# Four modulation tiles per load in the head of a two-layer trunk, and the mixed unit's tiles one by one

## The chip, the cores and the metric

The kernel runs on one core of a Trainium2 chip. The time is the device time of one execution in microseconds (us). The kernel before has a median of 2176.46 us over three runs (2176.29 to 2176.57).

The core has TensorE (PE; its weight loads are shown as PEld), VectorE (DVE), ScalarE (ACT), GpSimd (POOL) and SyncE (SP). In this kernel all loads and stores are issued by SyncE, and 16 DMA engines carry them.

## What is computed

A trunk of two layers on 256 tokens of width 2048, in float32. Each layer has a mixer (layer 0 pools over windows, layer 1 is a gated linear recurrence) and a SwiGLU FFN, and both are modulated by six vectors that come from one conditioning vector c:

```
cond = jax.nn.silu(c)
for layer in range(DEPTH):
    mod = cond @ w_ada[layer] + b_ada[layer]
    sh_m, sc_m, g_m, sh_f, sc_f, g_f = jnp.split(mod[:, None, :], N_MOD, axis=-1)
    h = rms_norm(x, norm_mix_gain[layer]) * (1.0 + sc_m) + sh_m
    ...
    x = x + g_m * y
    h = rms_norm(x, norm_ffn_gain[layer]) * (1.0 + sc_f) + sh_f
    x = x + g_f * swiglu(h, w_ffn_in[layer], w_ffn_out[layer])
return rms_norm(x, final_gain)
```

`w_ada` has 2048 rows and 12288 columns per layer, 100.7 MB each, as much as a large part of the other weights. It is used for one row vector, so its cost is bringing it in and multiplying it once.

## The kernel before

**Units.** `w_ada` is cut into units of 2048 rows x 1024 columns (half a section; the mixed units take 512 columns of the FFN's shift and 512 of its scale). A unit is 16 tiles of 128 rows x 1024 columns, 512 KB each; tile k holds rows 128k to 128k+127. Seven units are worked off in the head, ahead of the main loop, in the order of `HEAD`: scale, shift, scale, shift of the first mixer (units 0 to 3), its gate in two halves (units 4, 5) and the mixed unit (unit 6). Seventeen more are spread through the main loop (`BEHIND`).

**Who works on a unit.** In the head, TensorE takes the first tiles of each unit (`PE_LOADS`: 7, 7, 7, 6, 8, 8, 9 of the 16) in `multiply_loads`, line 665: two products per tile, which the trace shows as four rows of 128x512. VectorE folds the rest in `fold`, lines 1343 (first) and 1346 (the others), each as tile times cond plus the accumulator. Line 1340 adds TensorE's row to VectorE's accumulator. Then TensorE sums over the partitions (`sum_columns`, line 672, after `head_columns`, line 683, or `reduce_unit`, line 699, for the gates) and ScalarE copies the result (line 990 or 997). Between the units stand the pooling matmuls (lines 766, 767), the products with the pooling weights (lines 637 to 639) and the residual updates. The main loop begins with the first FFN product, at 178.25 us in the trace.

**The ring of tiles.** The head's tiles go to a ring of 16 slots (tile n to slot n mod 16): slots 0 to 3 are `ada`, slots 4 to 15 are `ada_head`. SyncE issues the loads in program order. For each pair of tiles (n even) it waits until both slots are free (`ada_free`, counted up by TensorE or VectorE when they have read a tile) and issues one DMA of 1 MB, line 429. In HBM the two tiles lie so that each partition's 8 KB are contiguous. One semaphore per pair tells the arrival; both tiles' consumers wait for it (`ada_arrived`). SyncE's order in the head: parameters; unit 0 (the bias rows `brows` behind its fourth tile); x; units 1 and 2; two pooling weight tiles; unit 3; two more; unit 4; four more and `pscale`; unit 5; two FFN weight tiles; unit 6. Behind the head, tiles come one by one to `ada`, line 425, 4 KB per partition, from the same array, between the weight tiles (line 405), which are 512 KB and contiguous.

## Time and profile before

| | |
|---|---|
| median of three runs | 2176.46 us (2176.29 to 2176.57) |
| the profiled execution | 2179.37 us, span 2177.7 us |
| TensorE busy | 2130.3 us, 98% of the span |
| VectorE busy | 1641.1 us, 75% |
| ScalarE busy | 998.0 us, 46% |
| moved by DMA | 574.34 MB, mean 264 GB/s |
| the head (0 to 178 us) | DMA share 0.97, 399 GB/s; TensorE busy 152.41 us |

Busy times are of one execution. Times in the traces are us from the span's start. The DMA share is the mean busy share of the 16 engines, and it stands at 1.01 or 1.02 where they never pause, since packets of an engine overlap a little. The granted clock is TensorE's, as a share of 2.4 GHz.

### The profile page before, as it was taken

The numbers are of one execution on the slowest core, as the hardware profiler recorded it, in microseconds if no ns is written. First come the engines' busy times: TensorE is split into PE (matmuls) and PEld (weight loads), VectorE is DVE, ScalarE is ACT, GpSimd is POOL, SyncE is SP. The second block draws the span as 40 slices with busy tenths as digits, with TensorE's granted clock in tenths as the row PEclk, the third lists the DMA queues.
The fourth block names the chain that finished last, engine by engine and source line by source line (L and its number), as shares of the span: only waits on it lengthen the run. The fifth ranks groups of instructions, "written<-read, shape, count | busy, mean of one in ns | idle before, by whom it ended". The sixth has DMA issues, their size and how long they took to land.

```text
span 2177.7 us, 24635 instructions
## 1 busy us (share of the span) xinstructions
PE 2130.3 (98%) x9513; PEld 1724.8 (79%) x9513; DVE 1641.1 (75%) x1685; ACT 998.0 (46%) x1116; POOL 21.0 (1%) x89
## 2 busy tenths in 40 slices
PE   7999999999999999999999999999999999999997
PEld 3557887888888888878888888878888888888886
DVE  5779899999988887769787887677756666546644
ACT  2324544444444334455655566554454444444433
POOL 1000000000000000010000000000000000000000
PEclk9999999999999999999999999999999999999999
DMA  9998898988899998756666664578856556558664
GB/s 383 418 418 336 326 345 295 322 319 315 311 339 331 340 338 290 251 181 231 217 202 213 222 199 160 191 281 300 280 185 192 185 182 187 193 188 297 236 216 136
DMA packets 149105, 574.34 MB, mean 264 GB/s; under 512 B 16662, under 2 KB 16854, under 8 KB 141308
## 3 DMA queue, kind: packets, MB, share of 16 engines
q1 hardware_dynamic: 148988, 572.77, 74.6%
q8 instruction: 75, 1.23, 0.2%
q14 instruction: 42, 0.34, 0.0%
HBM read 570.60 MB, written 2.10 MB: 263 GB/s over the span
## 4 chain that ended last, share of the span: by engine, by line
PE 91%; DVE 4%; issue 2%; DMA 1%; ACT 1%; SPq 0%; DVEq 0%; ACTq 0%
PE prod L637 28%; PE prod L639 28%; PE prod L638 28%; DVE acc L1346 2%; PE modp L665 2%; PE small L708 1%; DMA ada<-in_ada_sections 1%; PE small L880 1%; PE modp L672 1%; DMA ada_head<-in_ada_sections 1%; PE modp L699 1%; PE small L855 0%; DVE part_value L1642 0%; PE small L901 0%; PE small L865 0%
## 5 line engine op out<-in xcount | busy, mean ns | idle before, releaser
L964 ACT ACTIVATE w_hi<-raw 128x1024 fp32r<-128x1024 f32 x696 | 736.0, 1061 | 988.9 <-PE prod L639 908.3
L1297 DVE TENSOR_TENSOR w_lo<-raw,w_hi 128x1024 fp32r<-128x1024 f32 x696 | 848.3, 1222 | 420.7 <-ACT w_hi L964 419.2
L637 PE MATMUL prod<-w_hi,h_hi 128*128 128x512 f32 x2072 | 818.9, 395 | 4.9 <-issue 1.9
L639 PE MATMUL prod<-w_hi,h_lo 128*128 128x512 f32 x2072 | 808.3, 390 | 0.0
L638 PE MATMUL prod<-w_lo,h_hi 128*128 128x512 f32 x2072 | 808.1, 390 | 0.0
L637 PEld LDWEIGHTS prod<-w_hi,h_hi 128*128 128x128 f32 x2072 | 390.1, 188 | 86.7 <-issue 3.1
L639 PEld LDWEIGHTS prod<-w_hi,h_lo 128*128 128x128 f32 x2072 | 389.9, 188 | 82.0
L638 PEld LDWEIGHTS prod<-w_lo,h_hi 128*128 128x128 f32 x2072 | 390.3, 188 | 79.0 <-issue 1.0
L1346 DVE SCALAR_TENSOR_TENSOR acc<-ada,cond,acc 128x1024 f32<-128x1024 f32 x255 | 326.1, 1279 | 0.4
L637 PE MATMUL prod<-w_hi,g_hi 128*128 128x512 f32 x688 | 268.8, 391 | 0.0
L639 PE MATMUL prod<-w_hi,g_lo 128*128 128x512 f32 x688 | 267.7, 389 | 0.0
L638 PE MATMUL prod<-w_lo,g_hi 128*128 128x512 f32 x688 | 267.7, 389 | 0.0
L637 PEld LDWEIGHTS prod<-w_hi,g_hi 128*128 128x128 f32 x688 | 129.2, 188 | 27.3 <-issue 0.5
L638 PEld LDWEIGHTS prod<-w_lo,g_hi 128*128 128x128 f32 x688 | 129.2, 188 | 27.1 <-issue 0.5
L639 PEld LDWEIGHTS prod<-w_hi,g_lo 128*128 128x128 f32 x688 | 129.1, 188 | 26.7
L665 PE MATMUL modp<-ada,cond_rows 128*128 128x512 f32 x112 | 57.3, 671 | 10.3 <-DMA brows<-in_b_ada 6.8
L665 PEld LDWEIGHTS modp<-ada,cond_rows 128*128 128x128 f32 x112 | 23.7, 217 | 40.5 <-issue 35.1
L708 PE MATMUL small<-ident,tok 128*128 128x128 f32 x272 | 37.3, 282 | 7.0 <-issue 4.8
L708 PEld LDWEIGHTS small<-ident,tok 128*128 128x128 f32 x272 | 32.8, 145 | 13.8 <-issue 6.9
L665 PE MATMUL modp<-ada_head,cond_rows 128*128 128x512 f32 x96 | 42.3, 592 | 0.0
L1346 DVE SCALAR_TENSOR_TENSOR acc<-ada_head,cond,acc 128x1024 f32<-128x1024 f32 x29 | 37.2, 1284 | 4.4 <-DMA ada_head<-in_ada_sections 2.0
L1046 ACT ACTIVATE feat<-small,mod,gain 128x256 f32<-128x256 f32 x48 | 23.4, 563 | 29.5 <-PE small L708 27.0
(196 smaller groups left out, 1051.9 us busy)
## 6 DMA issues: line engine op xcount, KB each, us to landing
raw<-in_w_ffn_in SPq DMA_DIRECT2D x352, 512.0 KB, 4.6
ada<-in_ada_sections SPq DMA_DIRECT2D x256, 512.0 KB, 5.9
raw<-in_w_ffn_out SPq DMA_DIRECT2D x176, 512.0 KB, 4.3
raw<-in_hgrn_w_in SPq DMA_DIRECT2D x128, 512.0 KB, 3.6
ada_head<-in_ada_sections SPq DMA_DIRECT2D x36, 1024.0 KB, 15.7
raw<-in_hgrn_w_out SPq DMA_DIRECT2D x32, 512.0 KB, 3.5
ada<-in_ada_sections SPq DMA_DIRECT2D x12, 1024.0 KB, 12.0
ada<-in_ada_mixed SPq DMA_DIRECT2D x16, 512.0 KB, 7.3
```

The source lines that it names most:

```text
L637: pe.matmul(o, hi[:, k, ts], wh, start=(begin and s == 0), stop=False)
L638: pe.matmul(o, hi[:, k, ts], wl, start=False, stop=False)
L639: mm = pe.matmul(o, lo[:, k, ts], wh, start=False, stop=(end and s == n - 1))
L665: mm = pe.matmul(modp[:, o], cond_rows[:, k], ada_buffer(slot)[:, o * CH:(o + 1) * CH], start=(k == 0), stop=(in_columns(u) and k == n_row ...
L672: mm = pe.matmul(modp[:, 0, j:j + 1], a[:, j * P:(j + 1) * P], ones[:, 0:1], start=False, stop=(j == UB - 1))
L699: mm = pe.matmul(modp[:, o], ones[:, :], a[:, o * CH:(o + 1) * CH], start=not begun, stop=True)
L708: mm = pe.transpose(small[half][:, o:o + P], block_of(tb, 2 * half + j), ident[:, :])
L880: mm = pe.matmul(small[b][:, o:o + P], kdec[:, b, pair, ts], kdec[:, b, 2 + pair, ts], start=True, stop=True)
L964: act.activation(w_hi[:, slot], raw[:, r], ACT.Copy).then_inc(hi_ready, 1)
L1046: ins = act.activation(feat[:, half, j], small[half][:, j * S:(j + 1) * S], ACT.Identity, bias=shifts[:, k:k + 1], scale=gains[:, k:k + 1])
L1297: dve.tensor_tensor(w_lo[:, slot], raw[:, r], w_hi[:, slot], ALU.subtract).then_inc(lo_ready, 1)
L1346: ins = dve.scalar_tensor_tensor(a, ada_buffer(slot), cond[:, k:k + 1], a, ALU.mult, ALU.add)
```

## The change

For units 0 to 5 of the head one load brings four tiles (2 MB, 16 KB per partition in one piece) instead of two. SyncE waits for four free slots before it issues, and consumers of any of the four tiles wait for the whole load. The mixed unit (unit 6) is loaded tile by tile, 4 KB per partition, as the units behind the head are; each of its tiles has its own semaphore. For this the arrays in HBM are laid out in groups of four tiles, so that a single tile's rows lie 16 KB apart from partition to partition (8 KB before). That holds for the 16 tiles of every single-tile unit, in the main loop too.

```
-    sections = w.reshape(L, D // (2 * P), 2, P, 6, 2, D // 2).transpose(0, 4, 5, 1, 3, 2, 6)
-    mixed = w[0, :, 3 * D:5 * D].reshape(D // (2 * P), 2, P, 2, D // CH, CH)[:, :, :, :, 0:2].transpose(4, 0, 2, 1, 3, 5)
-    return sections, mixed.reshape(2, D // (2 * P), P, 2, 2 * CH)
+    sections = w.reshape(L, D // (4 * P), 4, P, 6, 2, D // 2).transpose(0, 4, 5, 1, 3, 2, 6)
+    mixed = w[0, :, 3 * D:5 * D].reshape(D // (4 * P), 4, P, 2, D // CH, CH)[:, :, :, :, 0:2].transpose(4, 0, 2, 1, 3, 5)
+    return sections, mixed.reshape(2, D // (4 * P), P, 4, 2 * CH)
...
-            if n < len(HEAD) * KD:
-                slot -= slot % 2
-            elif slot % 2:
-                before -= len(HEAD) * KD // ADA_HEAD
+            if n < (len(HEAD) - 1) * KD:
+                slot -= slot % 4
+            elif slot % 4:
+                before -= len(HEAD) - 1
...
-                if u >= len(HEAD):
+                if u >= len(HEAD) - 1:
                     sp.wait_ge(ada_free[slot], before)
-                    sp.dma_start(ada_buffer(slot), tiles[k // 2, :, k % 2]).then_inc(ada_loaded[slot], 16)
-                elif k % 2 == 0:
-                    for tile in range(2 if before else 0):
+                    sp.dma_start(ada_buffer(slot), tiles[k // 4, :, k % 4]).then_inc(ada_loaded[slot], 16)
+                elif k % 4 == 0:
+                    for tile in range(4 if before else 0):
                         sp.wait_ge(ada_free[slot + tile], before)
-                    sp.dma_start(ada_pair(slot).rearrange("p k n -> p (k n)"),
-                                 tiles[k // 2].rearrange("p k n -> p (k n)")).then_inc(ada_loaded[slot], 16)
+                    sp.dma_start(ada_four(slot).rearrange("p k n -> p (k n)"),
+                                 tiles[k // 4].rearrange("p k n -> p (k n)")).then_inc(ada_loaded[slot], 16)
```

No instruction of TensorE, VectorE or ScalarE is added, removed or moved; what they wait for changes. On SyncE the loads are merged.

VectorE in unit 0, the folds of tiles 7 to 14 and the row that adds TensorE's sum. `ada_loadedN` is the semaphore of the load that brings slot N and its followers, `ada_freeN` tells that slot N has been read. Before:

```order
L1343 TENSOR_SCALAR acc<-ada_head,cond 128x1024 [waits ada_loaded6,cond_ready]
L1346 SCALAR_TENSOR_TENSOR acc<-ada_head,cond,acc 128x1024 [waits ada_free7,ada_loaded8]
L1346 SCALAR_TENSOR_TENSOR acc<-ada_head,cond,acc 128x1024 [waits ada_free8,ada_loaded8]
L1346 SCALAR_TENSOR_TENSOR acc<-ada_head,cond,acc 128x1024 [waits ada_free9,ada_loaded10]
L1346 SCALAR_TENSOR_TENSOR acc<-ada_head,cond,acc 128x1024 [waits ada_free10,ada_loaded10]
L1346 SCALAR_TENSOR_TENSOR acc<-ada_head,cond,acc 128x1024 [waits ada_free11,ada_loaded12]
```

The same folds now:

```order
L1343 TENSOR_SCALAR acc<-ada_head,cond 128x1024 [waits ada_loaded4,cond_ready]
L1346 SCALAR_TENSOR_TENSOR acc<-ada_head,cond,acc 128x1024 [waits ada_free7,ada_loaded8]
L1346 SCALAR_TENSOR_TENSOR acc<-ada_head,cond,acc 128x1024 [waits ada_free8,ada_loaded8]
L1346 SCALAR_TENSOR_TENSOR acc<-ada_head,cond,acc 128x1024 [waits ada_free9,ada_loaded8]
L1346 SCALAR_TENSOR_TENSOR acc<-ada_head,cond,acc 128x1024 [waits ada_free10,ada_loaded8]
L1346 SCALAR_TENSOR_TENSOR acc<-ada_head,cond,acc 128x1024 [waits ada_free11,ada_loaded12]
```

The folds are the same and in the same order; the wait of tile 8 (`ada_loaded8`) is now for a load of tiles 8 to 11, and tile 7 waits for tiles 4 to 7.

SyncE between unit 2's last loads and unit 3's first ones, before:

```order
L429 DMA ada_head<-in_ada_sections 128x2048 [waits ada_free13,ada_free12]
L429 DMA ada_head<-in_ada_sections 128x2048 [waits ada_free15,ada_free14]
L405 DMA raw<-in_pool_w 128x1024 x2
L429 DMA ada<-in_ada_sections 128x2048 [waits ada_free1,ada_free0]
L429 DMA ada<-in_ada_sections 128x2048 [waits ada_free3,ada_free2]
L429 DMA ada_head<-in_ada_sections 128x2048 [waits ada_free5,ada_free4]
```

And now:

```order
L429 DMA ada_head<-in_ada_sections 128x4096 [waits ada_free14,ada_free15,ada_free13,ada_free12]
L405 DMA raw<-in_pool_w 128x1024 x2
L429 DMA ada<-in_ada_sections 128x4096 [waits ada_free2,ada_free3,ada_free1,ada_free0]
L429 DMA ada_head<-in_ada_sections 128x4096 [waits ada_free6,ada_free7,ada_free5,ada_free4]
L429 DMA ada_head<-in_ada_sections 128x4096 [waits ada_free10,ada_free11,ada_free9,ada_free8]
```

Two issues have become one, and the first load of unit 3 waits for slots 0 to 3, where it waited for 0 and 1.

## Rows read from the trace of the kernel before

**Rows 1.** The page: the span, and busy time of each engine.
```profile
span 2177.7 us, 24635 instructions
...
PE 2130.3 (98%) x9513; PEld 1724.8 (79%) x9513; DVE 1641.1 (75%) x1685; ACT 998.0 (46%) x1116; POOL 21.0 (1%) x89
```

**Rows 2.** Stretches (us): busy time per engine, granted clock, DMA share, rate.
```profile
core 0: us, PE busy (x) PEld busy (x) DVE busy (x) ACT busy (x) POOL busy (x), PEclk, DMA share, GB/s
...
178.00:460.00 282.00, 278.75 (x1226) 227.46 (x1227) 263.67 (x260) 134.12 (x140) 0.00 (x0) 0.99 0.88 324
...
20.00:40.00 20.00, 16.09 (x47) 9.89 (x46) 11.36 (x10) 5.31 (x16) 0.00 (x0) 0.77 1.01 421
60.00:78.00 18.00, 15.28 (x50) 7.96 (x49) 16.75 (x23) 2.11 (x2) 0.00 (x0) 1.00 1.01 418
...
280.00:300.00 20.00, 20.00 (x90) 16.30 (x89) 18.49 (x21) 8.35 (x8) 0.00 (x0) 1.00 1.01 393
282.00:298.00 16.00, 16.00 (x72) 12.97 (x71) 14.49 (x17) 6.33 (x7) 0.00 (x0) 1.00 1.02 399
```

**Rows 3.** Instructions in order of time, VectorE, head: start, us, what, [idle before].
```profile
18.57 9.62 DVE L1346 SCALAR_TENSOR_TENSOR acc<-ada_head,cond,acc 128x1024 f32<-128x1024 f32 x7 [1.67 <-DMA ada_head<-in_ada_sections]
...
43.50 1.29 DVE L1346 SCALAR_TENSOR_TENSOR feat<-ada_head,cond,feat 128x1024 f32<-128x1024 f32 x1 [1.20 <-DMA ada_head<-in_ada_sections]
...
55.45 1.28 DVE L1346 SCALAR_TENSOR_TENSOR feat<-ada_head,cond,feat 128x1024 f32<-128x1024 f32 x1
```

**Rows 4.** Instructions in order of time, TensorE, head.
```profile
30.86 3.57 PE L672 MATMUL modp<-ones,acc 128*128 128x1 f32 x16 [0.93 <-DVE acc L1346]
...
36.00 9.57 PE L665 MATMUL modp<-ada,cond_rows 128*128 128x512 f32 x16
...
57.44 0.39 PE L683 MATMUL modp<-ident,brows 64*128 64x8 f32 x2
...
62.27 7.03 PE L665 MATMUL modp<-ada,cond_rows 128*128 128x512 f32 x16
...
127.15 7.11 PE L665 MATMUL modp<-ada,cond_rows 128*128 128x512 f32 x16 [1.92 <-DMA ada<-in_ada_sections]
...
154.87 7.13 PE L665 MATMUL modp<-ada,cond_rows 128*128 128x512 f32 x16 [1.11 <-ACT gate L990]
...
178.25 0.77 PE L637 MATMUL prod<-w_hi,h_hi 128*128 128x512 f32 x1 [1.90 <-issue]
```

**Rows 5.** The chain that ended last, in order of time: start, us, what.
```profile
107.81 19.21 DMA ada<-in_ada_sections
```

**Rows 6.** Instructions in order of time, ScalarE, before unit 5.
```profile
125.27 1.02 ACT L990 ACTIVATE gate<-modp 128x1024 f32<-128x1024 f32 x1 [21.29 <-PE modp L699]
```

**Rows 7.** The DMA view of the whole span: instruction queue, and a lone load's landing.
```profile
q8 instruction: 75, 1.23, 0.2%
...
raw<-in_hgrn_w_out SPq DMA_DIRECT2D x32, 512.0 KB, 3.5
```

**Rows 8.** Stretches of half granted clock, columns as in rows 2.
```profile
30.70:41.00 10.30, 10.14 (x30) 7.31 (x31) 1.31 (x3) 6.29 (x18) 0.00 (x0) 0.50 1.01 421
...
78.50:85.30 6.80, 6.53 (x15) 3.87 (x16) 2.20 (x4) 3.93 (x9) 0.00 (x0) 0.50 1.02 417
...
174.10:184.30 10.20, 8.30 (x26) 6.96 (x26) 8.36 (x14) 4.49 (x8) 0.00 (x0) 0.50 0.40 121
```

**Rows 9.** SyncE in order of time; DMA view of 65.5:67 and of 137:149.
```profile
65.94 3.76 SPq L429 DMA_DIRECT2D ada<-in_ada_sections x2
...
137.77 10.80 SPq L429 DMA_DIRECT2D ada_head<-in_ada_mixed x6
...
ada<-in_ada_sections SPq DMA_DIRECT2D x1, 1024.0 KB, 11.0
...
ada_head<-in_ada_mixed SPq DMA_DIRECT2D x6, 1024.0 KB, 18.7
```

**Rows 10.** DMA view of 278:300: weight tiles, and single modulation tiles.
```profile
raw<-in_w_ffn_in SPq DMA_DIRECT2D x9, 512.0 KB, 6.3
ada<-in_ada_sections SPq DMA_DIRECT2D x9, 512.0 KB, 5.9
```

More of the change, by code:

```diff
@@ L369, in ada_buffer, with ada_four @@
             return ada[:, slot] if slot < ADA else ada_head[:, slot - ADA]
-        def ada_pair(slot):
-            return ada[:, slot:slot + 2] if slot < ADA else ada_head[:, slot - ADA:slot - ADA + 2]
+        def ada_four(slot):
+            return ada[:, slot:slot + 4] if slot < ADA else ada_head[:, slot - ADA:slot - ADA + 4]
         def ada_arrived(eng, n):
             slot, before = ada_slot(n)
-            if n < len(HEAD) * KD:
-                slot -= slot % 2
-            elif slot % 2:
-                before -= len(HEAD) * KD // ADA_HEAD
+            if n < (len(HEAD) - 1) * KD:
+                slot -= slot % 4
+            elif slot % 4:
+                before -= len(HEAD) - 1
             eng.wait_ge(ada_loaded[slot], 16 * (before + 1))
```

## The prediction, made before the changed kernel ran

> **What bounds the kernel now.** I read the page's first lines, then the stretches. The profiled execution took 2179.37 us with a span of 2177.7, so 1.7 us lie around the span [rows 1]; the three timed runs have their median at 2176.46, 2.9 us below it. I work with differences inside the trace and add the result to 2176.46. TensorE is busy for 98% of the span [rows 1]. From 178.25 us, where the first product of the first FFN starts, it hardly stops: 278.75 of 282 us between 178 and 460 [rows 2]. What the head (0 to 178 us) gains or loses, the end gains or loses too, as long as nothing else changes behind it.
>
> The head has two candidates. The first is the stream of transfers: its share stands at 1.01 (full, with rounding) at 418 to 421 GB/s [rows 2]. The second is the chain of compute, each unit's tiles multiplied by TensorE, then folded by VectorE, then summed into columns or rows. A reader who stops at the share of 1.01 takes the stream for the bound. The waits say otherwise. Where does somebody on the chain wait for a transfer? In unit 0, VectorE starts its eight remaining folds at 18.57, 1.67 us after its first, on a transfer; in unit 1 it waits until 43.50, but TensorE's own work (28 matmul rows from 36.00, then the pooling matmuls) runs to 57.44 while VectorE ends its last fold at 55.45 + 1.28 = 56.7, so TensorE is last there; at 127.15 TensorE waits 1.92 us for the first load of unit 5 [rows 3, 4]. The chain of work that ended last shows that load in it: issued at 107.81, landed 19.21 us later, at 127.02 [rows 5]. But the gate copy on ScalarE, which TensorE also needs there, ends at 125.27 + 1.02 = 126.29 [rows 6]. So only about 0.8 us of this wait can be won even if the transfer came at once. Units 6 and the rest wait on no transfer: TensorE starts unit 6 at 154.87 on the gate copy [rows 4]. The head is thus a chain of compute that touches the stream at 18.57 and, barely, at 127.15.
>
> **The change, part by part.**
>
> *Coarser arrival, a loss.* A consumer of tile 8 of a unit waited for tiles 8 and 9; now it waits for 8 to 11. The stream is in the same order and full, so this is one more megabyte (1.0486 MB at 421 GB/s [rows 2]): 2.49 us. In unit 0 VectorE has nothing else to do there, and it is on the chain: 18.57 becomes 21.06 before any gain of rate. Its eight folds then run back to back, because four folds of 1.37 us (9.62 us for 7) take 5.5 us and the next load comes after 5.0.
>
> *Larger packets, a gain.* The trace has no data transfer with packets of 16 KB, so I bound it. Packets of 8 KB at 418 GB/s take 16 x 8192 / 418 = 313.6 ns on each of 16 engines; in the stretches of full share with packets of 4 KB the rate is 393 and 399 GB/s, or 166.8 and 164.3 ns [rows 2]. So 4 KB more cost 147 to 149 ns, and a packet of 16 KB on the same line takes 607 to 612 ns, 15 to 20 ns less than two of 8 KB. One load is 8 such packets on each engine: 0.12 to 0.16 us saved per load, of which I take 0.14. The ends for the range are 0.16 us saved, and on the other side the only 16 KB packets there are, those of the instruction queue: 75 packets in 0.2% of 16 engines' time, 0.002 x 16 x 2177.7 / 75 = 0.93 us each [rows 7]. I stay by the line through 4 and 8 KB, since those rows are the same kind of transfer to the same memory; the instruction packets go elsewhere and share their engine with the data.
>
> *Sum at unit 0.* 2.49 less 3 loads x 0.14 = 0.42: **+2.1 us** on VectorE at the end of unit 0, and so on TensorE's column sums at 30.86 and its multiplications of unit 1 at 36.00 [rows 4]. From 30.7 to 41.0 the granted clock is at half (1.2 of 2.4 GHz) [rows 8]. If it rises again at the same time, unit 1 starts 2.1 us later but has 2.1 us less of half speed, which leaves +1.0. If it rises later, since TensorE was idle for longer before, it costs up to half of 3.5 us (the difference between the shortest and the longest such stretch [rows 8]) more: +2.8. I take **+2.0** at 57.44. VectorE's own branch in unit 1 goes from 43.50 by 2.49 less 7 x 0.14 = +1.5, to 58.2 at its end; TensorE, at 59.4, is still last.
>
> *At unit 5.* The shift of 2.0 is carried through units 2 to 4, which are compute from end to end. TensorE could start unit 5 at 126.3 + 2.0 = 128.3. The load lands at 127.02 + 2.49 - 21 x 0.14 = 126.6. So the wait for it goes, the chain's own shift takes its place, and the start moves from 127.15 to about 128.3: **+1.2**. This is the heart of it: the gain of rate (2.9 us by then) pays for the coarser arrival at unit 5, where there was almost nothing to win, and the price at unit 0 stays.
>
> *Coarser issue.* SyncE waits for four free tiles instead of two before it issues. The tightest place is unit 3: its first pair was issued at 65.94 and landed 11.0 us later, so the stream reached it at 76.9 - 2.5 = 74.4 [rows 9]. Now the issue waits for four tiles of unit 2 on TensorE, 62.27 + 7.03 + 2.0 = 71.3 [rows 4], while the stream, 12 loads x 0.14 = 1.7 earlier, would come to it at 72.7. A lead of 1.4 us. A lone load of 512 KB lands 3.5 us after its issue [rows 7], 2.2 us more than its own 1.3 us; so the stream may stand still there for up to 0.8 us. That is hidden: the stream is 1.7 us ahead of TensorE at unit 5 by the numbers above. Cost 0, with 0.8 us for the high end. Queued behind that wait on SyncE are only the next loads of the same ring.
>
> *The mixed unit tile by tile.* Eight loads of 1 MB become sixteen of 512 KB, at 393 to 399 instead of 418 GB/s: 8.39 MB take 1.0 to 1.3 us longer. The loads of before were issued from 137.77 and landed a median 18.7 us later [rows 9], TensorE came to the unit at 154.87 on the gate, so the cover is some microseconds, and the stream is 3.4 us earlier by then (24 x 0.14). Eight more issues on SyncE at some 0.4 us each lie in waits for free tiles. Cost 0.
>
> *Wider rows behind the head.* The single tiles of 256 + 16 loads are now read at a pitch of 16 KB between partitions, before 8 KB. At 8 KB pitch such loads land in 5.9 us beside 6.3 for the weights, which are contiguous [rows 10]: no price of the pitch can be seen, and there is no row for 16 KB. The Trainium skill (DMA: Bandwidth & Descriptors, Latency and other measured facts) warns that rows a large power of two apart lose rate, 207 GB/s at a pitch of 512 KiB, and advises contiguous tiles. No run here shows such a pitch; by that rule 16 KB is far from the case, and the four-tile loads themselves are contiguous. I take 0.
>
> *Start of the main loop.* It starts at 178.25 in a stretch at half clock (174.1 to 184.3) [rows 4, 8]. A start 1.2 us later with the same end of the stretch loses 0.6. I leave +1.0, between.
>
> **Forecast:** 2176.46 + 1.0 = 2177.5 us.
>
> **The rivals.**
>
> *The fixed cost of each load counts (faster).* A lone load shows 2.2 us beyond its transfer [rows 7]. Sections go from 48 loads to 24, the mixed unit from 8 to 16: 16 fewer, times 2.2 = 35 us, to 2141. Against it: loads that are queued land 2.5 us apart at full share, so this cost is overlapped. The Trainium skill (DMA: Bandwidth & Descriptors, Anatomy of one DMA) gives per load about 2.0 us plus bytes at 436 GB/s, for GpSimd's path, and its 16 times 2.0 would be 32 us; the share of 1.01 contradicts it here as a serial cost. Chance 0.01. *A gain in TensorE's clock (faster):* both later stretches at half would have to shrink away, worth half of TensorE's 6.5 us and of its 6 us in the main loop there, 6 us together less the 1.0: 2171. Chance 0.04.
>
> *Packets of 16 KB are slower than two of 8 (slower).* The place is the first load of unit 5. Without any gain of rate it lands at 129.5, 2.4 us later than now; 168 packets per engine come before it ends, so from 11 ns of extra time per packet (638 against 627 ns) the kernel is over 4.4 us slower. At the instruction queue's 0.93 us it would be 24 x 8 x 0.3 = 58 us, to 2234. For it speaks only that row, against it the straight line of the two sizes measured. Chance 0.11, most of it near the decision point.
>
> *No gain of rate (the rows are cut into packets of 8 KB, or the stream is at a ceiling).* Only the price of coarser arrival is left: +2.4 at unit 5, 2178.9, and with the clock's 1.7 us and the 0.8 of the queue 2181.4. Chance 0.14; it counts as no change.
>
> **How the numbers follow.** 0.2% (4.4 us) is about what a measurement of this kernel tells from no change. My forecast, 0.70, and the case without a gain of rate, 0.14, lie within it: 0.84. Faster is 0.05, slower 0.11. The low end is the forecast with the third half-clock stretch gone (3 us) and the whole gain of rate: 2173.5; the high end is the case without gain and with its extras: 2181.5.
>
> **What would show it.** In the changed kernel: data packets of 16 KB in the page; VectorE's folds of unit 0 starting tile 8 near 20.6 us instead of 18.57; TensorE's wait for a transfer before unit 5 gone, with its start near 128; the stream at 427 to 432 GB/s between 20 and 120 us; the first product of the FFN near 179; full share all the way to 150 us. Wrong would be: a rate below 418, a hole in the DMA share near 73 us of more than 1 us, a half-clock stretch that begins or ends elsewhere, or any difference behind 184 us.

## The result, and the profile after

| | before | after |
|---|---|---|
| median, us | 2176.52 (2176.14 to 2179.03) | 2184.65 (2181.43 to 2186.85) |
| ratio to before | | 1.0031, 95% interval 1.002 to 1.0043 |
| the profiled execution | 2179.37, span 2177.7 | 2184.07, span 2182.3 |
| first product of the first FFN | 178.25 [rows 4] | 183.02 |

The change costs 8.1 us by the medians, 6.7 us by the ratio, and 4.7 us between the two profiled executions. Timed once more beside the kernel before (`changed_again` below) it costs 6.2 us by the medians. The forecast was +1.0 and the range ended at 2181.5: the prediction was wrong in size, and the kernel is slower where no change, within 4.4 us, was held likeliest. In the profiled pair the head holds all of it: the main loop starts 4.8 us later and the span is 4.6 us longer.

The page of the kernel after (span; busy time per engine with share and count), against [rows 1]. TensorE is busy for 1.2 us more with the same 9513 instructions, VectorE and ScalarE as before: something is waited for.

```profile
span 2182.3 us, 24611 instructions
...
PE 2131.5 (98%) x9513; PEld 1725.1 (79%) x9513; DVE 1640.8 (75%) x1685; ACT 998.0 (46%) x1116; POOL 21.0 (1%) x89
```

VectorE in order of time, after, against [rows 3]: start, us, what, idle before it and what ended that. These are unit 0 (first row), the end of unit 1 (one) and unit 3 (two).

```profile
21.35 9.62 DVE L1346 SCALAR_TENSOR_TENSOR acc<-ada_head,cond,acc 128x1024 f32<-128x1024 f32 x7 [4.08 <-DMA ada_head<-in_ada_sections]
...
57.90 1.28 DVE L1346 SCALAR_TENSOR_TENSOR feat<-ada_head,cond,feat 128x1024 f32<-128x1024 f32 x1
...
92.96 9.62 DVE L1346 SCALAR_TENSOR_TENSOR feat<-ada_head,cond,feat 128x1024 f32<-128x1024 f32 x7 [2.65 <-DMA ada_head<-in_ada_sections]
...
103.91 1.28 DVE L1346 SCALAR_TENSOR_TENSOR feat<-ada_head,cond,feat 128x1024 f32<-128x1024 f32 x1
```

The same two steps of unit 3 before, which the prediction did not look at:

```profile
86.94 9.62 DVE L1346 SCALAR_TENSOR_TENSOR feat<-ada_head,cond,feat 128x1024 f32<-128x1024 f32 x7 [0.27 <-DMA ada_head<-in_ada_sections]
...
97.89 1.28 DVE L1346 SCALAR_TENSOR_TENSOR feat<-ada_head,cond,feat 128x1024 f32<-128x1024 f32 x1
```

Unit 0's tile 8 starts at 21.35 (18.57 before). Unit 3's starts at 92.96, 6.0 us later than before, and VectorE's last fold there, which ended at 99.2, well ahead of TensorE, now ends at 105.2.

TensorE in order of time, after, against [rows 4]. These are the column sums of unit 0, unit 1, the column sums of unit 1, one of the pooling matmuls behind them, units 2 and 3, the bias row and the column sums of unit 3, and units 4, 5 and 6.

```profile
33.64 3.58 PE L672 MATMUL modp<-ones,acc 128*128 128x1 f32 x16 [0.73 <-DVE acc L1346]
...
38.79 8.52 PE L665 MATMUL modp<-ada,cond_rows 128*128 128x512 f32 x16
...
59.49 1.95 PE L672 MATMUL modp<-ones,feat 128*128 128x1 f32 x16
...
63.23 1.06 PE L766 MATMUL small<-band,xs 128*128 128x256 f32 x2
...
65.67 7.03 PE L665 MATMUL modp<-ada,cond_rows 128*128 128x512 f32 x16
...
82.78 8.72 PE L665 MATMUL modp<-ada,cond_rows 128*128 128x512 f32 x16 [0.27 <-ACT mod L997]
...
103.93 0.39 PE L683 MATMUL modp<-ident,brows 64*128 64x8 f32 x2 [0.92 <-DVE feat L1340]
105.25 2.47 PE L672 MATMUL modp<-ones,feat 128*128 128x1 f32 x16 [0.93 <-DVE feat L1346]
107.99 9.76 PE L665 MATMUL modp<-ada,cond_rows 128*128 128x512 f32 x16 [0.27 <-ACT mod L997]
...
132.94 7.13 PE L665 MATMUL modp<-ada,cond_rows 128*128 128x512 f32 x16 [1.11 <-ACT gate L990]
...
160.66 7.13 PE L665 MATMUL modp<-ada,cond_rows 128*128 128x512 f32 x16 [1.11 <-ACT gate L990]
```

The same places in units 3 and 4 before:

```profile
80.55 9.50 PE L665 MATMUL modp<-ada,cond_rows 128*128 128x512 f32 x16 [0.27 <-ACT mod L997]
...
101.50 0.39 PE L683 MATMUL modp<-ident,brows 64*128 64x8 f32 x2
101.82 1.95 PE L672 MATMUL modp<-ones,feat 128*128 128x1 f32 x16
104.03 7.13 PE L665 MATMUL modp<-ada,cond_rows 128*128 128x512 f32 x16 [0.27 <-ACT mod L997]
```

| TensorE starts | unit 1 | unit 2 | unit 3 | unit 4 | unit 5 | unit 6 | main loop |
|---|---|---|---|---|---|---|---|
| before | 36.00 | 62.27 | 80.55 | 104.03 | 127.15 | 154.87 | 178.25 |
| after | 38.79 | 65.67 | 82.78 | 107.99 | 132.94 | 160.66 | 183.02 |
| later by | 2.8 | 3.4 | 2.2 | 4.0 | 5.8 | 5.8 | 4.8 |

The shift doesn't grow evenly. At unit 3 it is back at 2.2 us, and it grows behind that: the bias row and the column sums of unit 3 now wait 0.92 and 0.93 us for VectorE, and unit 4 takes 9.76 us instead of 7.13.

SyncE's loads of units 3 to 5 in order of time, after, against [rows 9]:

```profile
72.79 0.33 SPq L429 DMA_DIRECT2D ada<-in_ada_sections  x1
77.99 2.94 SPq L429 DMA_DIRECT2D ada_head<-in_ada_sections  x3
91.59 0.33 SPq L429 DMA_DIRECT2D ada<-in_ada_sections  x1
95.00 10.61 SPq L429 DMA_DIRECT2D ada_head<-in_ada_sections  x3
117.85 0.33 SPq L429 DMA_DIRECT2D ada<-in_ada_sections  x1
```

The DMA view of 117 to 125 us gives the landing of that last load (unit 5's first): 14.7 us after its issue, so at 132.55.

```profile
ada<-in_ada_sections SPq DMA_DIRECT2D x1, 2048.0 KB, 14.7
```

Stretches, columns as in [rows 2]: first three of after, the last one of before for comparison with the second.

```profile
20.00:66.00 46.00, 38.98 (x138) 25.50 (x137) 30.46 (x40) 14.92 (x36) 0.00 (x0) 0.85 1.01 426
66.00:90.00 24.00, 21.39 (x59) 10.32 (x58) 16.51 (x16) 6.04 (x11) 0.00 (x0) 0.93 0.90 358
72.00:76.00 4.00, 4.00 (x11) 1.74 (x10) 3.69 (x4) 2.11 (x2) 0.00 (x0) 1.00 0.61 188
```

```profile
66.00:90.00 24.00, 21.01 (x55) 10.56 (x54) 18.07 (x17) 6.04 (x11) 0.00 (x0) 0.86 1.02 419
```

Full stretches run at 426 instead of 419 GB/s, but between 72 and 76 us the stream stands still for over a third of the time, and over 66 to 90 it brings 358 instead of 419 GB/s: (419 - 358) x 24 / 419 = 3.5 us of stream are lost.

Stretches of half granted clock, after, against [rows 8]:

```profile
31.40:41.60 10.20, 8.55 (x30) 6.91 (x31) 3.91 (x5) 4.19 (x12) 0.00 (x0) 0.50 1.01 430
62.10:65.50 3.40, 3.40 (x12) 2.87 (x12) 3.12 (x11) 0.00 (x0) 0.00 (x0) 0.50 1.03 439
82.60:86.00 3.40, 3.22 (x4) 1.51 (x5) 0.33 (x2) 3.17 (x8) 0.00 (x0) 0.50 1.03 395
...
106.50:113.30 6.80, 6.53 (x14) 3.35 (x14) 5.06 (x13) 0.18 (x1) 0.00 (x0) 0.50 1.01 429
181.60:188.40 6.80, 5.38 (x13) 4.25 (x14) 6.01 (x10) 3.79 (x6) 0.00 (x0) 0.50 0.46 153
```

In sum 30.6 us instead of 27.3, so only 1.7 us of full speed more. But two of them, near 62 and 107 us, lie where TensorE is the last to finish.

In the main loop both executions have the same low clock between 925 and 940 us, 0.77 (first row before, second after). The third row is of `pairs_in_fours`, a run below that takes the time of before:

```profile
925.00:940.00 15.00, 11.29 (x46) 8.85 (x46) 11.04 (x21) 7.71 (x14) 11.04 (x30) 0.77 0.03 10
925.00:940.00 15.00, 11.30 (x43) 8.59 (x42) 10.23 (x24) 6.87 (x16) 11.25 (x30) 0.77 0.15 52
925.00:940.00 15.00, 11.80 (x57) 10.05 (x58) 12.14 (x24) 9.33 (x19) 12.45 (x27) 0.89 0.16 48
```

The chain of work that ended last, in order of time, after. Before, it went through the load of unit 5 [rows 5]; now it goes through one of unit 3 and VectorE's folds behind it (in the second trace of the changed kernel through both loads).

```profile
78.47 14.46 DMA ada_head<-in_ada_sections
...
105.25 2.49 PE modp L672 x16
107.99 16.63 PE modp L665 x32
```

### The profile page after: what moved, and what is told of

Read it like the earlier page. It is cut to its first block, busy times and chain, and to the rows that moved or that the text cites. A ratio compares the mean times of both kernels' runs of the same rounds, so it can differ in the third digit from the quotient of the medians.

```text
span 2182.3 us, 24611 instructions
## 1 busy us (share of the span) xinstructions
PE 2131.5 (98%) x9513; PEld 1725.1 (79%) x9513; DVE 1640.8 (75%) x1685; ACT 998.0 (46%) x1116; POOL 21.0 (1%) x89
## 4 chain that ended last, share of the span: by engine, by line
PE 91%; DVE 4%; issue 2%; DMA 1%; ACT 1%; SPq 0%; ACTq 0%; DVEq 0%
PE prod L637 28%; PE prod L639 28%; PE prod L638 28%; PE modp L665 3%; DVE acc L1346 2%; DMA ada_head<-in_ada_sections 1%; PE small L708 1%; PE small L880 1%; PE modp L699 1%; PE small L855 0%; DVE feat L1346 0%; PE modp L672 0%; DVE part_value L1642 0%; PE small L901 0%; PE small L865 0%
## 5 line engine op out<-in xcount | busy, mean ns | idle before, releaser
L637 PEld LDWEIGHTS prod<-w_hi,g_hi 128*128 128x128 f32 x688 | 129.2, 188 | 27.3 <-issue 0.5
```

Source lines behind the costliest of these rows:

```text
L637: pe.matmul(o, hi[:, k, ts], wh, start=(begin and s == 0), stop=False)
```

## The experiments

Theories. **A**: the loss is the coarser arrival at the places where somebody waits for a load. **Q**: it is the coarser issue, which lets the stream stand still. **P**: it is the layout (packets, pitch). **C**: it is TensorE's clock. Each experiment is the changed kernel with its loads written so that three numbers per head unit can be set: tiles per load, free slots that SyncE waits for, and tiles that must have landed before any of them is used. HBM keeps groups of four throughout.

```
-                if u >= len(HEAD) - 1:
-                    sp.wait_ge(ada_free[slot], before)
+                size, wide = (SIZE[u], ISSUE[u]) if u < len(HEAD) else (1, 1)
+                for tile in range(wide if before and k % wide == 0 else 0):
+                    sp.wait_ge(ada_free[slot + tile], before)
+                if size == 1:
...
-                elif k % 4 == 0:
...
+                elif k % size == 0:
```

With 4, 4, 4, 4, 4, 4, 1 in all three lists this is the change itself. It was timed again as `changed_again`, beside unit0_by_two, only_unit0_by_four and changed_filled:

> The changed kernel once more, written with a table of sizes per unit (the same instructions), as the measure for the three others on the same chip. Expected: 5 to 8 us slower than before. Its second profile shows whether the hole in the stream near 74 us and TensorE's extra half-clock stretches (62.1 to 65.5 and 106.5 to 113.3 us in the first) come again. Theory A (late arrival in unit 0 shifts the chain, and the extra half-clock stretches follow from it): both extra stretches again, within a few us of the same places.

Measured: 2184.49 us (2184.01 to 2186.03), ratio 1.0034 (1.0021 to 1.0046). That is 6.2 us over the 2178.26 of before beside it, as expected. The two half-clock stretches of which the expectation speaks come again (62.9 to 66.3 and 107.3 to 110.7), and the stream over 66 to 90 us runs at 381 GB/s, where the first execution has 358: 2.2 us lost instead of 3.5. In this execution the load is the last to come at unit 5, at 132.49:

```profile
132.49 7.10 PE L665 MATMUL modp<-ada,cond_rows 128*128 128x512 f32 x16 [2.31 <-DMA ada<-in_ada_sections]
```

So at unit 5 two things are late together, the load (about 132.5 in both executions) and the chain of compute (gate copy until 132.88 in the first, 131.24 in the second).

**The layout alone.** Loads of two tiles, in every head unit, from arrays in groups of four: 8 KB packets, and the pitch of 16 KB behind the head.

```
+    AHEAD, SIZE, ISSUE, ARRIVE = 4, [2, 2, 2, 2, 2, 2, 2], [2, 2, 2, 2, 2, 2, 2], [2, 2, 2, 2, 2, 2, 2]
```

> The layout alone: arrays in groups of four tiles as in the changed kernel, but every unit of the head in loads of two tiles (8 KB per partition, taken from rows 16 KB apart), issue and arrival by two as before; the mixed unit in pairs as well. Theory Q (the queue runs dry: waiting for four free tiles leaves the stream without work at unit 3, and VectorE's folds there become last): the time of before, 2176.5 within 1 us, and a head stream of 416 to 421 GB/s. Theory A (coarse arrival: consumers wait for four tiles, and TensorE's half-clock stretches follow from that): the same. Theory P (the 16 KB pitch or the larger packets cost rate): slower, by 1 us or more, and single loads in the main loop land later than 5.9 us.

Measured: 2176.91 us against 2178.46 for before, ratio 0.9997 (0.9988 to 1.0006). The single loads of the main loop land in a median 5.7 us (5.9 before). The pitch costs nothing. P, as far as it is the pitch, falls. Its other half, the packets of 16 KB, was not run alone: no run has them without the coarser arrival.

**Coarse issue alone.** Two tiles per load, but SyncE waits for four free slots at every fourth tile.

```
+    AHEAD, SIZE, ISSUE, ARRIVE = 4, [2, 2, 2, 2, 2, 2, 1], [4, 4, 4, 4, 4, 4, 1], [2, 2, 2, 2, 2, 2, 1]
```

> Loads of two tiles that each have their own semaphore and consumers who wait for two, but SyncE waits for four free slots before it issues two loads (units 0 to 5); the mixed unit tile by tile. Theory Q: the hole in the stream near 72 to 76 us is there (DMA share under 0.8), VectorE starts tile 8 of unit 3 at 90 us or later instead of 86.9, and the kernel is 2 to 5 us slower than before. Theory A: no change, within 1 us of before. Theory P: no change.

Measured: 2176.76 us, ratio 0.9994 (0.9985 to 1.0002). SyncE issues unit 3's first load at 69.57 (65.94 before) and the stream does not notice. The stretch of 66 to 90 us:

```profile
66.00:90.00 24.00, 21.01 (x55) 10.51 (x54) 18.18 (x17) 6.05 (x11) 0.00 (x0) 0.86 1.02 420
```

Q alone falls: 2 to 5 us were expected of it.

**Coarse arrival alone.** Two tiles per load and two free slots per issue, but consumers wait for four tiles.

```
+    AHEAD, SIZE, ISSUE, ARRIVE = 4, [2, 2, 2, 2, 2, 2, 1], [2, 2, 2, 2, 2, 2, 1], [4, 4, 4, 4, 4, 4, 1]
```

> Loads of two tiles, issued when two slots are free, but consumers wait for the load that ends their group of four (units 0 to 5); the mixed unit tile by tile. Theory Q: VectorE starts tile 8 of unit 0 near 21 us, TensorE's start of unit 1 moves by 2 to 3 us, no hole in the stream, and the kernel is 1 to 3 us slower (the first load of unit 5 arrives 2.5 us later, without the gain of rate). Theory A: 5 us or more slower, as the changed kernel. Theory P: no change.

Measured: 2181.99 us (2178.76 to 2184.65), ratio 1.0019 (1.001 to 1.0028). Unit 5, and the stretch of 66 to 90:

```profile
131.31 8.50 PE L665 MATMUL modp<-ada,cond_rows 128*128 128x512 f32 x16 [2.69 <-DMA ada<-in_ada_sections]
...
66.00:90.00 24.00, 21.40 (x59) 10.29 (x58) 16.94 (x16) 6.05 (x11) 0.00 (x0) 0.93 1.00 397
```

Over half of the loss, 4.1 us by the ratio (2.2 to 6.1), is there with the loads of before; that lies between what Q (1 to 3 us) and A (5 or more) expected. And the stream already runs at 397 there: tiles used late are freed late, so it loses (419 - 397) x 24 / 419 = 1.3 us with the issue still by two. The changed kernel loses 3.5 and 2.2 us there in its two traces. It differs from this run by two things, the issue by four and the single load of 2 MB; loads of two with issue and arrival by four, which would separate them, was not run. That the issue has a part is read from the trace: SyncE issues unit 3's first load at 72.79 (69.46 in this run), and the share of 72 to 76 us is 0.61. Here VectorE is not the last at unit 3: the column sums there start at 103.54 without a wait.

**Which unit pays.** Single units go back to two tiles (all three lists alike), or single units alone go to four.

```
+    AHEAD, SIZE, ISSUE, ARRIVE = 4, [4, 4, 4, 2, 4, 4, 1], [4, 4, 4, 2, 4, 4, 1], [4, 4, 4, 2, 4, 4, 1]
```

> The changed kernel with unit 3 alone in loads of two tiles (issue and arrival by two there). Theory Q: the stream is full through 66 to 90 us, VectorE starts tile 8 of unit 3 before 88 us, and the kernel is within 2.5 us of before, so 4 us or more of the loss are gone. Theory A: it stays 5 us or more slower than before, as units 0, 1, 2, 4 and 5 still arrive by four. Theory P: it stays slower too.

```
+    AHEAD, SIZE, ISSUE, ARRIVE = 4, [2, 4, 4, 4, 4, 4, 1], [2, 4, 4, 4, 4, 4, 1], [2, 4, 4, 4, 4, 4, 1]
```

> The changed kernel with unit 0 alone in loads of two tiles. Theory A0 (unit 0's late arrival is the root of the shift and of the extra half-clock stretches): tile 8 of unit 0 at 18.7 us, TensorE's unit 1 near 36.2, no half clock near 62 and near 107 us, and the kernel within 2 us of before. Theory A1 (every unit's arrival by four costs, unit 0 is one of six): half or less of the loss goes, 3 us or more stay.

```
+    AHEAD, SIZE, ISSUE, ARRIVE = 4, [4, 2, 2, 2, 2, 2, 1], [4, 2, 2, 2, 2, 2, 1], [4, 2, 2, 2, 2, 2, 1]
```

> Only unit 0 in loads of four tiles, units 1 to 5 in loads of two, the mixed unit tile by tile. Theory A0: slower than before by 3 us or more, with half-clock stretches near 62 and near 107 us. Theory A1: at most 2 us slower.

```
+    AHEAD, SIZE, ISSUE, ARRIVE = 4, [4, 4, 4, 4, 4, 2, 1], [4, 4, 4, 4, 4, 2, 1], [4, 4, 4, 4, 4, 2, 1]
```

> The changed kernel with unit 5 alone in loads of two tiles. Theory W (TensorE's wait for the first load of unit 5 decides what of the earlier shifts reaches the end: 2.3 to 3.5 us of it in the runs so far): the wait falls by up to 2.4 us, to 1 us or less, and the kernel is 1 to 3 us faster than the changed one, 3 to 5 us slower than before. Rival (the shifts of compute and clock from units 0 to 4 carry the loss by themselves): within 1 us of the changed kernel's 6 us over before.

```
+    AHEAD, SIZE, ISSUE, ARRIVE = 4, [2, 4, 4, 2, 4, 2, 1], [2, 4, 4, 2, 4, 2, 1], [2, 4, 4, 2, 4, 2, 1]
```

> Units 0, 3 and 5 in loads of two tiles, units 1, 2 and 4 in loads of four. By theory W with unit 0's own price (2.2 us when alone) all three places where somebody on the chain waits for an arrival are as before: within 1.5 us of before, stream at 415 GB/s or more between 66 and 90 us. Rival: units 1 and 2 by four alone open the hole and delay VectorE, 2 us or more slower than before.

```
+    AHEAD, SIZE, ISSUE, ARRIVE = 4, [2, 4, 4, 2, 2, 2, 1], [2, 4, 4, 2, 2, 2, 1], [2, 4, 4, 2, 2, 2, 1]
```

> Only units 1 and 2 in loads of four. Theory W: within 1 us of before. Rival (VectorE in unit 1 starts its second fold 2 us later at 45.7 and becomes last there, which moves unit 2 by 1 us): 1 us or more slower, with unit 2 on TensorE at 63.5 instead of 62.3.

Measured, with the start of unit 5 on TensorE in the profiled execution, what released it, and the rate over 66 to 90 us:

| kernel | units by four | median, us | before beside it | ratio (95%) | unit 5 starts | GB/s |
|---|---|---|---|---|---|---|
| changed_again | 0 to 5 | 2184.49 | 2178.26 | 1.0034 (1.0021 to 1.0046) | 132.49, load | 381 |
| unit0_by_two | 1 to 5 | 2183.79 | 2178.26 | 1.0027 (1.0018 to 1.0037) | 130.44, load | 407 |
| unit3_by_two | 0, 1, 2, 4, 5 | 2182.86 | 2178.46 | 1.0018 (1.0009 to 1.0027) | 131.26, load | 384 |
| unit5_by_two | 0 to 4 | 2179.76 | 2176.75 | 1.0013 (1.0004 to 1.0022) | 129.22, gate copy | 398 |
| units035_by_two | 1, 2, 4 | 2179.83 | 2176.75 | 1.001 (1.0002 to 1.0019) | 127.68, gate copy | 418 |
| units12_by_four | 1, 2 | 2180.17 | 2176.75 | 1.0011 (1.0002 to 1.002) | 129.32, gate copy | 388 |
| only_unit0_by_four | 0 | 2180.49 | 2178.26 | 1.001 (1.0001 to 1.0019) | 129.25, gate copy | 408 |

The largest single step is unit 5: its loads by two take the ratio from 1.0034 to 1.0013, some 4.6 us (3.2 by the medians over before; the intervals just touch), and its first load is no longer waited for:

```profile
129.22 7.10 PE L665 MATMUL modp<-ada,cond_rows 128*128 128x512 f32 x16 [1.17 <-ACT gate L990]
```

Part of that difference may be the execution: nothing that unit 5's loads can touch differs ahead of 105 us, and yet this execution has no half-clock stretch near 62 or 107 us, where the other has two. Unit 3 by two gives 1.6 thousandths back with the intervals overlapping, and does not help at unit 5 (2.72 us of wait for the load): theory A's place at unit 3 is real on VectorE (tile 8 at 87.76 instead of 92.96) but mostly not on the path then. The stream is not full either (384 GB/s), where Q expected it to be and 4 us of the loss to go. Unit 0 by two (unit0_by_two) takes both extra half-clock stretches away (none near 62 and 107 us in its trace), and the loss stays, 5.5 us by the medians: what A0 says of the loss falls. Nor do these stretches need unit 0: units12_by_four has both, only_unit0_by_four has neither. The profiled execution of unit0_by_two is the fastest of its nine (2180.59), so its trace shows less than the median's loss. Unit 0 alone costs 1.0010, 2.2 us (0.2 to 4.1), where the prediction had +2.0 behind unit 1 and +1.0 at the end. Units 1 and 2 alone cost as much, where the prediction had nothing. In unit 1, VectorE is last there, which moves the column sums by 1.5 us (its row in that kernel),

```profile
59.23 1.95 PE L672 MATMUL modp<-ones,feat 128*128 128x1 f32 x16 [0.93 <-DVE feat L1346]
```

the pooling matmuls behind it run at half clock, which makes it 3.0 us at unit 2 (65.29), and the stream runs at 388 GB/s, as unit 2's tiles are used and freed later. With units 0, 3 and 5 by two the stream is whole again (418 GB/s), unit 5 starts 0.5 us later than before, and one thousandth of loss stays. That is 2.2 us where W expected at most 1.5, and the trace doesn't show where: its execution, 2177.18 us, is the fastest of eleven. The parts, 1.0 for unit 0, 1.1 for units 1 and 2 and the 2.1 that unit 5 takes back, make 4.2 thousandths of a whole of 3.4; each is uncertain by about one, so whether they add up is not shown.

**The other way: finer.** Units 0 and 5 tile by tile.

```
+    AHEAD, SIZE, ISSUE, ARRIVE = 4, [1, 2, 2, 2, 2, 1, 1], [1, 2, 2, 2, 2, 1, 1], [1, 2, 2, 2, 2, 1, 1]
```

> The other way: units 0, 5 and the mixed unit tile by tile (4 KB per partition), units 1 to 4 in loads of two. Theory W: VectorE starts tile 8 of unit 0 about 1 us earlier than before (17.6 instead of 18.6), TensorE's unit 1 follows by up to 1 us, the first load of unit 5 lands about when it did (1.2 us sooner for being one tile, 1 us later for 4 KB packets in unit 0), and the kernel is 0 to 1.5 us faster than before. Rival (packets of 4 KB cost the stream more than the finer arrival brings): 0 to 2 us slower.

Measured: 2179.12 us (2176.61 to 2180.45), ratio 1.0005 (0.9996 to 1.0013). No gain. VectorE gets tile 8 of unit 0 at 17.77 (18.57 before), and still unit 5 starts at 126.78 on its load:

```profile
17.77 9.62 DVE L1346 SCALAR_TENSOR_TENSOR acc<-ada_head,cond,acc 128x1024 f32<-128x1024 f32 x7 [0.46 <-DMA ada_head<-in_ada_sections]
...
126.78 7.10 PE L665 MATMUL modp<-ada,cond_rows 128*128 128x512 f32 x16 [1.83 <-DMA ada<-in_ada_sections]
```

It reaches the main loop 0.4 us earlier than before (177.81), too little to be measured. So nothing tried here beats two tiles per load: four lose, and one, tried at units 0 and 5, gains nothing.

**TensorE's clock.** Products whose result nobody reads are put where TensorE only waits. First around the column sums of unit 0 in the changed kernel, three ahead of the bias row and one behind it:

```
+            def fill(n):
+                for _ in range(n):
+                    pe.matmul(prod[1][:, 0], ones[:, :], cond_rows[:, 0:4].rearrange("p a n -> p (a n)"), start=True, stop=True)
...
+                fill(3 if u in (0,) else 0)
...
+                fill(1 if u in (0,) else 0)
```

> The changed kernel, and TensorE gets four more products of 128x128 by 128x512 in unit 0, where it waits for VectorE (three before the column bias, one before the column sums), into a PSUM bank that nobody reads before it is written anew. They add 3.6 us of work at full clock to a wait of 5.3 and one of 0.7 us. Theory C (the granted clock decides the size of the loss): the half clock from 31.4 to 41.6 us starts later or is shorter, unit 1 ends 2 us or more earlier than in the changed kernel, and the kernel is 2 us or more faster than it. If the clock has no part: the same time as the changed kernel, or up to 1 us slower from the added work.

Measured: 2184.37 us, ratio 1.003 (1.0018 to 1.0043). The half clock goes from 32.6 to 42.8, where the two traces of the changed kernel have 31.4 to 41.6 and 28.8 to 42.4. It starts later, but unit 1's last rows end at 53.4 instead of 52.5 and 52.8, and the time is that of `changed_again`, where C expected 2 us less. Then everywhere in the head:

```
+                fill({0: 3, 2: 3, 3: 3}.get(u, 0))
...
+                fill({0: 1, 2: 2, 3: 2, 6: 1}.get(u, 0))
...
+            evacuated(pe, 3)
             head_columns(6)
+            fill(2)
```

> The changed kernel with 13 extra products of 128x512 that nobody reads, in places where TensorE only waits: three ahead of the bias row of units 0, 2 and 3, then 1, 2, 2 and 1 between that row and the column sums of units 0, 2, 3 and 6, and two behind the mixed unit's column sums, where the wait for the result bank was moved ahead of the sums. The result is the reference's. Theory C (much of the loss is TensorE's clock falling to half near 62, 83, 107 and 182 us because of these waits, and comes back where they are filled): the stretches near 83, 107 and 182 us shrink or go, each worth up to 1.7 us, ratio to the kernel before near 1.001. Theory A (the loss is the waits for loads, and where half clock falls follows them): unit 5 still waits for its first load until about 132, whatever the clock does ahead of it, and at least 4 us of the loss stay: ratio 1.002 to 1.004.

Measured: 2185.01 us (2183.91 to 2187.41), ratio 1.004 (1.0026 to 1.0053). These are 17 products, not the 13 that the expectation counts. The clock partly does what C wants: no half clock between 80 and 90 us (1.00, where the changed kernel has 0.83), none from 100 to 110 (0.82), and 0.94 instead of 0.88 from 174 to 184. But a stretch of low clock (0.55) now stands at 111 to 114.8 us, again in unit 4. The time does not get better.

```profile
80.00:90.00 10.00, 9.73 (x36) 5.31 (x35) 4.97 (x6) 3.93 (x9) 0.00 (x0) 1.00 1.01 407
100.00:110.00 10.00, 10.00 (x44) 6.63 (x42) 7.58 (x7) 2.93 (x5) 0.00 (x0) 1.00 1.01 428
174.00:184.00 10.00, 9.31 (x40) 5.55 (x39) 8.92 (x9) 0.74 (x3) 0.00 (x0) 0.94 0.32 112
```

TensorE starts unit 4 at 110.73 (107.31 in changed_again) and unit 5 at 134.75, on the gate copy, not on the load, against A's expectation. So this run doesn't tell A from C cleanly: the products run over the waits that they fill. The same in the kernel before, first ten products (the expectation says nine), then three at the end only:

```
+                fill({0: 3, 2: 2}.get(u, 0))
...
+                fill({0: 1, 2: 1, 6: 1}.get(u, 0))
...
+            evacuated(pe, 3)
             head_columns(6)
+            fill(2)
```

> The kernel before with nine extra products of 128x512 that nobody reads: three ahead of the bias row of unit 0 and two ahead of unit 2's, one between that row and the column sums of units 0, 2 and 6, and two behind the mixed unit's column sums. The loads are as before. Theory C: the half-clock stretches at 30.7 to 41.0, 78.5 to 85.3 and 174.1 to 184.3 us shorten or go; the kernel takes 2 to 5 us less, ratio 0.998 to 0.999. Theory A (the clock in the head is cover for waits on VectorE and ScalarE, and a faster TensorE there only waits longer): only the stretch at the start of the main loop could pay, ratio 0.999 to 1.000.

```
+                fill({6: 1}.get(u, 0))
...
+            evacuated(pe, 3)
             head_columns(6)
+            fill(2)
```

> The kernel before with three of these products only: one between the bias row and the column sums of the mixed unit, two behind the sums. It tells the start of the main loop apart from the rest. Theory C: the half-clock stretch of 174.1 to 184.3 us gets shorter by 3 us or more and the time falls by 1 to 3 us, ratio 0.9988 to 0.9995. Theory A: the stretch begins because TensorE waited from about 162 on for the mixed unit's folds, which three products don't fill, and stays: ratio 1.000.

Measured, against 2177.05 us: 2176.43 (2174.45 to 2182.66), ratio 1.0 (0.9991 to 1.0008), and 2179.19 (2173.89 to 2181.26), ratio 1.0003 (0.9994 to 1.0011). In the profiled execution of the first, half clock turns up where before it was at full, near 62 and 106 us:

```profile
60.00:64.00 4.00, 4.00 (x14) 3.37 (x14) 3.62 (x12) 0.00 (x0) 0.00 (x0) 0.50 1.01 418
104.00:108.00 4.00, 3.73 (x7) 1.59 (x7) 3.14 (x12) 0.18 (x1) 0.00 (x0) 0.67 1.02 422
```

That execution takes 2180.31 us and is one of three of eleven at a mean granted clock of 0.990; the other eight have 0.994 or 0.995 and take 2174.5 to 2177.4. In the second, the profiled execution has full clock at the start of the main loop,

```profile
174.00:184.00 10.00, 9.93 (x46) 7.52 (x47) 9.16 (x14) 5.07 (x8) 0.00 (x0) 1.00 0.47 153
```

and takes 2175.49 us, 3.9 us less than the profiled execution of before. Yet its median is 2179.19: six of its eleven executions have a mean granted clock of 0.989 and take 2179.2 to 2181.3 us, three have 0.993 and take 2173.9 to 2175.5. No version here beats the kernel before by more than the measurement is uncertain.

## Why the prediction was wrong, step by step

*Coarser arrival at unit 0, +2.1 us.* Right in place, near in size: tile 8 at 21.35 instead of the 20.6 named, and the column sums of unit 1 at 59.49 instead of 57.76, +1.7 where +2.0 was taken for 57.44. Alone, unit 0 costs 2.2 us (0.2 to 4.1). *Larger packets.* Right in sign, too large: 426 to 429 GB/s in full stretches make 16 x 16384 / 427 = 614 ns a packet, 13 ns less than two of 8 KB, so 0.10 us per load and not 0.14. *Wider rows and the mixed unit.* Right: the pitch costs nothing (0.9997), and nobody waits for the mixed unit.

*The shift of 2.0 carried through units 2 to 4.* The first step that failed. It is 3.4 us at unit 2: 1.7 from unit 0, and 1.7 because the pooling matmuls ahead of it fall to half clock (1.06 us a pair instead of 0.60). Up to unit 3 that evens out: 2.2 us there, as the column sums of unit 2 take 1.95 us instead of 2.73. TensorE comes to the bias row of unit 3 only 1.5 us late (103.93 - 0.92 = 103.0, before 101.5). But the prediction, which took units 2 to 4 for compute from end to end, looked for waits on loads only where somebody had waited long before, and left out unit 3. There VectorE's tile 8 came with 0.27 us of wait, which means that it was just in time; now it starts 6.0 us later, and VectorE, which had been done 2.6 us ahead of TensorE's need, is last: +3.4 at the column sums, +4.0 at unit 4. Unit 4 then runs partly at half clock (9.76 us instead of 7.13) and the gate copy ends at 131.86 + 1.02 = 132.88, 6.6 us later than before.

*Coarser arrival in all.* The largest error by size. The prediction's sum gave the coarser arrival +1.2 us at unit 5, with the gain of the larger packets taken off, and +2.4 without that gain. Alone, with packets of 8 KB, it costs 4.1 us (2.2 to 6.1), and TensorE waits 2.69 us for the first load of unit 5 (start at 131.31 instead of 127.15).

*Coarser issue, cost 0.* The second error, in that the two edits were priced one by one. The changed kernel is 1.2 to 1.5 thousandths, about 3 us, slower than arrival by four alone, though the intervals overlap. The text put a lead of 1.4 us at unit 3, from a shift of 2.0, and priced only the first load. The shift there is 3.4, the issue came at 72.79 instead of 71.3, the stream stopped, and the second load waited again until 77.99. Coarse issue alone leaves the stream whole (420 GB/s over 66 to 90 us), coarse arrival alone takes little (397), and the changed kernel, with both, has 358 and 381 in its two traces. A lead of 1.4 us with 0.8 us of uncertainty was no cover, and the 0.8 us for the high end was too small: 3.5 and 2.2.

*The load of unit 5 lands at 126.6.* The heart of the forecast, and wrong by 6 us: 132.5. By the measured terms it is 127.0 + 2.5 for the coarser arrival - 21 x 0.10 for the packets + 3.5 for the hole = 130.9. Most of the other 1.6 us can be placed by what the stream had brought when the load had landed, before (first row) and after:

```profile
0.00:127.02 127.02, 105.87 (x337) 61.60 (x337) 80.47 (x102) 35.00 (x73) 9.12 (x59) 0.93 0.98 403
0.00:132.55 132.55, 108.57 (x337) 63.20 (x337) 79.80 (x101) 33.95 (x72) 9.12 (x59) 0.91 0.96 398
```

That is 51.2 and 52.8 MB, 1.6 MB more, of which the coarser arrival accounts for 1.05. So about 0.5 MB, some 1 us, of loads behind it had come in before its last piece; why is not shown. The start of unit 5 moved by 5.8 us, not by 1.2.

*Start of the main loop.* The shift does fall, from 5.8 to 4.8 us, but not as forecast. The forecast let the half-clock stretch end where it had ended, at 184.3; it lies at 181.6 to 188.4 instead, 6.8 us long instead of 10.2, and the column sums ahead of it, now at full clock, take 1.95 us instead of 2.96. The right sign here is luck.

Of the rivals, "slower" had the right sign by the wrong mechanism (packets of 16 KB are faster, not slower). The mechanism that decided, late use and coarse issue together emptying the stream, was named as what would be wrong ("a hole in the DMA share near 73 us of more than 1 us") and had no chance or price of its own. Both terms that were called small, the clock's 1.7 and the queue's 0.8, were counted only at the high end, and once each; the trace has half clock at two new places, and the hole is 2.2 to 3.5 us. (In the rival of slower packets, 2.4 us and 168 packets of 11 ns more are 4.2 us, so its border lies nearer to 12 ns. Nothing hangs on it.)

What stays open: how much of the 8.1 us is the clock. The profiled pair differs by 4.7 us and its half-clock stretches by 1.7; the medians differ by 3.4 us more than the pair, since the profiled execution of before was slower than any of its six timed ones. The trace of `pairs_in_fours`, 2176.92 us, shows where 2.5 us of these can lie: it reaches the main loop at 178.44 (178.25 before), but its clock is 0.66 instead of 0.50 from 174 to 184 us and 0.89 instead of 0.77 from 925 to 940, and its span is 2175.2 instead of 2177.7. The changed kernel has 0.77 and 0.78 from 925 to 940 in both traces. So against a typical execution of before part of the loss is clock, and some of it lies outside the head. Why the changed kernel falls to half clock more often was not shown.

## What to carry to other kernels

A ring of buffers ties the two sides together: whoever waits for more tiles uses them later, frees them later, and so issues the next load later. Price coarser loads as a round trip, at every place where a consumer arrives within one load's time of its data (a wait of 0.27 us is such a place), not only where it waits long today. Where the stream is full and the loads queue up, larger loads have little to give: here 0.1 us each, against 2.5 us of later arrival wherever one is waited for. And when executions of one kernel differ by several us, take more than one trace before a loss of that size is laid to one place: the hole was 3.5 us in one and 2.2 in the other.

## What the runs showed of the hardware

Queued loads of 2 MB with 16 KB per partition move 426 to 429 GB/s in full stretches, those of 1 MB with 8 KB 418 to 421. But `changed_again`, `unit5_by_two` and the two filled versions of the changed kernel have only 412 to 414 from 20 to 66 us, at a share of 1.00: between 48 and 56 us `changed_again` moves 369 to 381 GB/s at 0.97 to 1.00. What slows them there is not shown. Fewer loads did not save any fixed time that could be seen; the kernel has 16 fewer and is slower. A single tile read at a pitch of 16 KB between partitions costs no more than at 8 KB (ratio 0.9997).

Executions of one and the same kernel differ by 2 to 8 us, and with them the mean granted clock: before 2175.7 us at 0.993 and 2179.4 at 0.991, before_filled_end 2173.9 at 0.993 and 2181.3 at 0.989. In the traces the half-clock stretches lie at other places from execution to execution: of two executions of the changed kernel one has them at 106.5 to 113.3 us, the other at 107.3 to 110.7. More products of TensorE, put into its waits, moved these stretches about and left the median where it was.
